# Slots for expert weights given back in pieces before the first expert product, the residual products all behind it, one router product split around a transpose

## The reference

```python
h = h + mixer_block(rmsnorm(h, norm1_g[l]), ...)      # ends with: return merged @ w_o
h = h + hier_moe(rmsnorm(h, norm2_g[l]), w_group[l], w_router[l], w1[l], w3[l], w2[l])

# hier_moe: logits of 8 groups and 64 experts, the best group, its two best experts, then for each
return (jax.nn.silu(xb @ w1[e]) * (xb @ w3[e])) @ w2[e]
```

## Time and profile before

| | us |
|---|---|
| median of 3 runs | 1562.71 (1562.51 to 1564.31) |
| profiled execution, its own time | 1561.92 |
| its span | 1560.1 |
| PE busy in the span | 1263.3 (81%) |
| DMA share and rate, mean from 700 to 1500 us | 1.01, 428 GB/s |
| last landing of expert weights | 1551.5 |

### The profile page before, as it was taken

One profiled execution on the slowest core, in us unless ns is written; L12 is line 12 of the kernel. 1 busy time (PEld: TensorE's weight loads), 2 busy tenths in 40 slices (PEclk: granted clock), 3 DMA queues, 4 the chain that ended last, 5 costly groups with the idle time before them and its releaser, 6 DMA issues.

```text
span 1560.1 us, 16698 instructions
## 1 busy us (share of the span) xinstructions
PE 1263.3 (81%) x6953; PEld 642.1 (41%) x6953; DVE 516.9 (33%) x1096; ACT 228.8 (15%) x649; POOL 17.8 (1%) x30
## 2 busy tenths in 40 slices
PE   9999999999999999997676576577576576476577
PEld 4665644444588544543232232223233223223223
DVE  6554577785453674311011111111111111111101
ACT  2435213111122101211001001001001001001001
POOL 2000000000000000100000000000000000000000
PEclk9999999999999999999788888788888789788889
DMA  9531756405433449899999999999999999999997
GB/s 302 210 114 55 245 155 205 155 35 216 157 113 109 166 157 370 347 429 428 428 429 428 429 427 430 427 428 428 429 428 428 428 428 429 427 428 429 429 426 323
DMA packets 93419, 501.40 MB, mean 321 GB/s; under 512 B 6797, under 2 KB 34817, under 8 KB 68160
## 3 DMA queue, kind: packets, MB, share of 16 engines
q1 hardware_dynamic: 92608, 500.00, 78.9%
q0 software_dynamic: 768, 0.85, 0.3%
HBM read 499.78 MB, written 1.05 MB: 321 GB/s over the span
## 4 chain that ended last, share of the span: by engine, by line
PE 58%; DMA 39%; DVE 1%; issue 0%; SPq 0%; ACT 0%; DVEq 0%
DMA arena<-in_w 38%; PE ps L1630 17%; PE ps L1253 8%; PE ps L862 7%; PE ps L1505 6%; PE ps L1305 3%; PE ps L857 2%; PE ps L1067 2%; PE ps L1557 2%; PE ps L907 2%; PE ps L1437 2%; PE ps L1207 1%; DMA arena<-in_w_in 1%; PE ps L1375 1%; PE ps L1280 1%
## 5 line engine op out<-in xcount | busy, mean ns | idle before, releaser
L1630 PE MATMUL ps<-arena,hT 128*32 128x512 f32 x1984 | 276.9, 721 | 255.4 <-DMA arena<-in_w 255.4
L1630 PEld LDWEIGHTS ps<-arena,hT 128*32 128x32 f32 x1984 | 69.2, 130 | 462.6 <-issue 319.8
L2722 DVE TENSOR_TENSOR moe_hid<-moe_hid,ps 64x512 f32<-64x512 f32 x32 | 22.1, 690 | 482.8 <-ACT moe_hid L3090 482.8
L1652 PE MATMUL ps<-arena,moe_turned 128*32 128x512 f32 x1024 | 116.7, 595 | 28.0 <-DVE moe_turned L2724 27.8
L1610 PEld LDWEIGHTS ps<-sel,h 128*128 128x128 f32 x992 | 113.2, 192 | 24.1 <-issue 24.1
L1610 PE MATMUL ps<-sel,h 128*128 128x64 f32 x992 | 117.2, 276 | 0.0
L3090 ACT ACTIVATE moe_hid<-ps 64x512 f32<-64x512 f32 x32 | 18.8, 588 | 656.2 <-PE ps L1630 650.5
L862 PE MATMUL ps<-hT,arena 128*128 128x256 f32 x512 | 113.9, 380 | 0.1
L862 PEld LDWEIGHTS ps<-hT,arena 128*128 128x128 f32 x512 | 96.8, 190 | 15.0 <-issue 2.2
L3074 ACT ACTIVATE hT<-ps,gcol 128x64 f32<-128x64 f32 x252 | 55.0, 328 | 158.5 <-PE ps L1610 156.8
L1505 PE MATMUL ps<-arena 128*128 128x512 f32 x176 | 77.3, 593 | 0.0
(11 more groups left out here) (465 smaller groups left out, 1245.4 us busy)
## 6 DMA issues: line engine op xcount, KB each, us to landing
arena<-in_w SPq DMA_DIRECT2D x184, 2048.0 KB, 29.3
arena<-in_w_in SPq DMA_DIRECT2D x18, 2048.0 KB, 8.5
arena<-in_w_up SPq DMA_DIRECT2D x22, 1024.0 KB, 9.4
arena<-in_w SPq DMA_DIRECT2D x14, 1024.0 KB, 13.2
arena<-in_w_down SPq DMA_DIRECT2D x5, 2048.0 KB, 13.7
arena<-in_w_out SPq DMA_DIRECT2D x2, 2048.0 KB, 14.3
arena<-in_w_conv_out SPq DMA_DIRECT2D x2, 2048.0 KB, 7.8
arena<-in_w_attn_out SPq DMA_DIRECT2D x2, 2048.0 KB, 7.8
```

Of the source, the lines that this page charges most:

```text
L1630: last = mm(ps[k * CAP:(k + 1) * CAP, UP, :], x[:, c, (k % 2) * CAP:(k % 2 + 1) * CAP], w[:, at:at + DE], start=(c == 0), stop=(c == KC - 1))
L1652: last = mm(ps[k * CAP:(k + 1) * CAP, DN, :], a[:, m * 64 + (k % 2) * CAP:m * 64 + (k % 2 + 1) * CAP], w[:, at:at + 512], start=(m == 0), ...
```

## The change

It does five things.

1. The loads of slots 0, 1 and 2 are issued ahead of `wao0`, `wao1`, `wo0` and `wo1` and no longer behind them.
2. `mrg` is laid out by halves of the tokens, so that the part of half 0 is free after `wo(0, 1)`. A quarter of slot 9 is loaded from then on (behind a wait on `bank_filled`), and another quarter with the rest.
3. `wo(1, 1)` raises `dense_used` once more in its middle, so that the first half of `wo1`'s place (slot 8) can be loaded from then on; the counts that others wait for go up by one.
4. The residual of half 0 is no longer taken from `h_res` by two products between the router's, but from `h` by two more products behind `first_up` (`take_residual`). The rest of slot 10 waits for `h_turned` in place of `res_taken`.
5. Of the router product `logits(1, 0)` two chunks come ahead of `turn_h(1, 1)` and two behind it.

```diff
@@ SP queue
-            static_units(UNIT["downC"], len(UNITS))
+            static_units(UNIT["downC"], UNIT["wao0"])
...
                     sp.wait_ge(rms_ready, 8)
                     sp.wait_ge(h_moved, 4)
-                    sp.wait_ge(res_taken, 1)
+                    sp.wait_ge(h_turned, 4)
                 else:
-                    sp.wait_ge(dense_used, released(UNIT[{3: "wao0", 4: "wao1", 7: "wo0", 8: "wo1", 9: "wo1"}[at]]))
+                    sp.wait_ge(dense_used, released(UNIT[{3: "wao0", 4: "wao1", 7: "wo0", 8: "wo1", 9: "wo1"}[at]]) + (at >= 8))
...
+            for k in range(3):
+                moe_wait(0, k)
+                load_quarter(MOE_SLOTS[k], k)
+            static_units(UNIT["wao0"], len(UNITS))
             for pair in range(PAIRS):
-                for k in (0, 1, 2, 4, 5, 3) if pair in (1, 2) else range(UNITS_PAIR):
+                for k in (0, 1, 2, 4, 5, 3) if pair in (1, 2) else range(0 if pair else 3, UNITS_PAIR):
                     if (pair, k) == (1, 1):
-                        load_part(4, 1)
-                        load_part(5, 0)
+                        load_part(4, 2048, 4096)
+                        load_part(5, 0, 2048)
+                        sp.wait_ge(bank_filled, filled(PROD["wo_h0"], 1))
+                        load_part(4, 0, 1024)
                     if pair == 1 and k in (4, 5):
                         moe_wait(pair, k)
-                        load_part(k, k - 4)
+                        load_part(k, *((1024, 2048), (2048, 4096))[k - 4])
                         continue
...
+                    if (pair, k) == (1, 2):
+                        at = moe_slot(1, 2)
+                        sp.wait_ge(dense_used, released(UNIT["wo1"]))
+                        sp.dma_start(MOE_SLOTS[at][:, 0:2048], t["w3"][2, :, 0:2048]).then_inc(moe_loaded[at], 16)
+                        moe_wait(1, 2)
+                        sp.dma_start(MOE_SLOTS[at][:, 2048:4096], t["w3"][2, :, 2048:4096]).then_inc(moe_loaded[at], 16)
+                        continue
@@ PE: wo, logits, residual
-                    last = mm(ps[:, BANKS[step][n], :], mrg[:, c, half * P:(half + 1) * P], slot_view(u)[:, c, :],
+                    last = mm(ps[:, BANKS[step][n], :], mrg[:, half, c, :], slot_view(u)[:, c, :],
                               start=(c == 0), stop=(c == KC - 1))
+                    if half and n and c == 3:
+                        last.then_inc(dense_used, 1)
...
-            logits(1, 0)
+            logits(1, 0, (0, 1))
             turn_h(1, 1, (4, 3))
+            logits(1, 0, (2, 3))
             pe.wait_ge(assigned, 1)
...
+            def take_residual(half, n):
+
+                rows = h[:, half, :].rearrange("p (c n) -> p n c", c=KC)[:, n * 64:(n + 1) * 64, :]
+                mm(ps[:, 2 * half + n, :], ident, rows, start=True, stop=False, skip_group_check=True)
...
-            mm(ps[:, 0, :], ident, h_res[:, 0, 0:512], start=True, stop=False, skip_group_check=True)
...
-            mm(ps[:, 1, :], ident, h_res[:, 0, 512:1024], start=True, stop=False, skip_group_check=True).then_inc(res_taken, 1)
...
                 if p == 0:
-                    for n in range(2):
-                        rows = h[:, 1, :].rearrange("p (c n) -> p n c", c=KC)[:, n * 64:(n + 1) * 64, :]
-                        mm(ps[:, 2 + n, :], ident, rows, start=True, stop=False, skip_group_check=True)
+                    for half in range(2):
+                        for n in range(2):
+                            take_residual(half, n)
```

More of the change, by code:

```diff
@@ L391, in two_blocks @@
         w_sum_b = b1(4, 512)
-        mrg = xn2.rearrange("p a b -> p (a b)").rearrange("p (c s) -> p c s", c=KC)
+        mrg = xn2.rearrange("p h (c s) -> p h c s", c=KC)
         def down_at(i):
@@ L456, in moe_count @@
         def moe_count(slot, turn):
-            return 16 * turn + ((48 if turn == 1 else 64) if slot == 0 else 16 if slot in (1, 2, 3, 9, 10) else 0)
+            return 16 * turn + ((48 if turn == 1 else 64) if slot == 0 else 32 if slot == 9 else 16 if slot in (1, 2, 3, 8, 10) else 0)
         xg = hT[:, :, 0:2 * CAP]
@@ L562, in two_blocks @@
         piece_in = sem("piece_in")
-        quarter_used, res_taken = sem("quarter_used"), sem("res_taken")
+        quarter_used = sem("quarter_used")
         SEL_FIRST, SCATTERED_FIRST = PAIRS + 1, PAIRS + 1
@@ L706, in moe_wait, with load_part @@
                     sp.wait_ge(h_moved, 4)
-                    sp.wait_ge(res_taken, 1)
+                    sp.wait_ge(h_turned, 4)
                 else:
-                    sp.wait_ge(dense_used, released(UNIT[{3: "wao0", 4: "wao1", 7: "wo0", 8: "wo1", 9: "wo1"}[at]]))
-            def load_part(k, part):
+                    sp.wait_ge(dense_used, released(UNIT[{3: "wao0", 4: "wao1", 7: "wo0", 8: "wo1", 9: "wo1"}[at]]) + (at >= 8))
+            def load_part(k, lo, hi):
                 at = moe_slot(1, k)
-                sp.dma_start(MOE_SLOTS[at][:, part * 2048:(part + 1) * 2048], t["w2"][k - 2, :, part * 2048:(part + 1) * 2048]
-                             ).then_inc(moe_loaded[at], 16)
+                sp.dma_start(MOE_SLOTS[at][:, lo:hi], t["w2"][k - 2, :, lo:hi]).then_inc(moe_loaded[at], 16)
+            for k in range(3):
+                moe_wait(0, k)
+                load_quarter(MOE_SLOTS[k], k)
+            static_units(UNIT["wao0"], len(UNITS))
             for pair in range(PAIRS):
-                for k in (0, 1, 2, 4, 5, 3) if pair in (1, 2) else range(UNITS_PAIR):
+                for k in (0, 1, 2, 4, 5, 3) if pair in (1, 2) else range(0 if pair else 3, UNITS_PAIR):
                     if (pair, k) == (1, 1):
-                        load_part(4, 1)
-                        load_part(5, 0)
+                        load_part(4, 2048, 4096)
+                        load_part(5, 0, 2048)
+                        sp.wait_ge(bank_filled, filled(PROD["wo_h0"], 1))
+                        load_part(4, 0, 1024)
                     if pair == 1 and k in (4, 5):
                         moe_wait(pair, k)
-                        load_part(k, k - 4)
+                        load_part(k, *((1024, 2048), (2048, 4096))[k - 4])
                         continue
@@ L1566, in turn_h, with logits @@
                 last.then_inc(h_turned, 1)
-            def logits(half, n):
+            def logits(half, n, chunks=range(4)):
                 if n:
@@ L1575, in logits @@
                     pe.wait_ge(hT_act, 21 + half)
-                for c in range(4 * n, 4 * n + 4):
+                for c in (4 * n + k for k in chunks):
                     last = mm(ps[:, 6 - half, 0:NG + NE], hT[:, c, half * P:(half + 1) * P], router_w[:, c, :],
@@ L3043, in _ @@
                 act.wait_ge(m_turned, k + 1)
-                a_(mrg[:, 4 * n:4 * n + 4, half * P:(half + 1) * P], ps[:, bank, :].rearrange("p (c s) -> p c s", c=4),
+                a_(mrg[:, half, 4 * n:4 * n + 4, :], ps[:, bank, :].rearrange("p (c s) -> p c s", c=4),
                    ACT.Copy).then_inc(mrg_ready, 1)
```

## The result

| | before | changed |
|---|---|---|
| median of 10 runs each, us | 1563.03 (1562.22 to 1564.31) | 1567.95 (1566.1 to 1572.14) |
| profiled execution, its own time, us | 1561.92 | 1567.15 |
| its span, us | 1560.1 | 1565.4 |

The ratio is 1.0030, 95% interval 1.0022 to 1.0039. I had forecast 1562.2 (1560.8 to 1564.3), which is 0.5 us faster: wrong in sign, and the change is ten times that size. Timed again beside the experiments, the kernel before lay above 1565.5 in 20 of 96 runs, so the size of the loss is less sure than its sign.

The account below looks back on a forecast made before the run. Expert-weight reading was taken as the bound, with the 16th piece's landing deciding. Slot 4's later release (687.5 against 688.0) outweighed piece 12's 1.2 us, leaving -0.5 us: median 1562.2, range 1560.8 to 1564.3.

Parts of the forecast that it names:

- What bounds the kernel: Reading of expert weights from about 663 us: the end is the 16th piece's landing plus 863.5 plus 8.6 us.
- Slots 0 to 2 ahead of `wao0`: Early loads of 6.3 MB, moved from behind 592 to behind 544 us: gain 0, cost 0, 14.7 us become idle DMA.
- The cover: Second `wao` load, behind the early loads, would land at 576 to 577, 2.5 us ahead of DVE's need at 579.5.
- Pieces: Slots 8 to 10 in at about 657.6, not 662.2; gain given back before `first_up`, 0.8 us left at piece 12.
- The residual products: Two taken out of the router: 0.3 us gained ahead of `gather_first(1)`, 0 for L1679; both come back behind `first_up`.
- +3.63 us on PE ahead of slot 4: Four products behind `first_up` take 7.26 us, not 3.63; slot 4 issued at 679.7, piece 16 landing at 687.5, not 688.0.
- theory 2: Experiments' theory: the four products behind `first_up` delay slot 4's release by 3.5 us, more than its load's queue covers.
- The divided router product: In the router: `turn_h` 0.3 us earlier, but ACT's copy only ends at 650.8; gain 0.1 us (0 to 0.3).
- Slot 4 comes late: Rival at the 16th piece's issue: own load time above 8.3 us, up to 1.3 us slower, 1564.0; chance 0.13.
- front counts: Rival at 640 to 660 us: loads, not places, caused the gap; closing it gains 5.3 us, 1557.4; chance 0.07.
- cheap restart: Rival at slot 4: own load time below 7.1 us, the whole 1.2 us of piece 12 stay, 1561.5; chance 0.10.
- `wao` late: Rival at the second `wao` load: costs only from 2.5 us late, then hidden by 10; part of the remaining chance.

Follow-up runs that it names:

- e4: Kernel before with only the loads of slots 0 to 2 issued ahead of `wao0`; 1563.47 us, ratio 1.0000.
- e5: Changed kernel plus two filling products in PE's router waits, all four residual products moved behind `expert_down` of pair 0; 1563.51 us, ratio 0.9996.
- e8: Changed kernel plus one unneeded product of constants in PE's longer wait, for DVE's choice of experts; 1564.53 us, ratio 1.0006.
- e10: Changed kernel plus one filling product in PE's longer wait, all residual products behind `expert_down` of pair 0; 1563.53 us, ratio 0.9997.
- e9: Changed kernel plus one unneeded product only in the short wait ahead of the second `gather_first`, the longer wait left empty; 1570.4 us, ratio 1.0030.
- e1: Changed kernel plus two unneeded products of constants where the residual products of half 0 stood in the router; 1564.88 us, ratio 1.0006.
- e6: Kernel before with two more residual products behind `first_up` (those of half 1 done twice); 1564.21 us, ratio 1.0004.
- e3: Kernel before with only the residual of half 0 moved behind `first_up`, slot 10 waiting for `h_turned`; 1566.98 us, ratio 1.0031.
- e7: Kernel before with half 0's residual products moved from the router to behind `expert_down` of pair 0, slot 10 waiting for `h_turned`; 1567.27 us, ratio 1.0017.
- e2: Changed kernel with half 0's residual back between the router's products and slot 10's rest waiting for it; 1562.36 us, ratio 0.9993.
- e11: Kernel before with one filling product in PE's longer wait, all residual products late, slot 10 waiting for `h_turned`; 1564.12 us, ratio 1.0001.

## Why the prediction was wrong, point by point

- **What bounds the kernel.** Right. In all thirteen profiles the last landing follows the 16th by 862 to 865 us. The tail of 8.6 us is less fixed: 8.6 to 10.5.
- **Slots 0 to 2 ahead of `wao0`: gain 0, cost 0.** Right (e4: 1.0000). The idle DMA stands at 600 to 610 with 28 GB/s. The cover was thinner than I had it: the second `wao` load landed 10.3 us after its issue at 569.7, at 580.0, and DVE used it at 581.3, 1.3 us later and not 2.5.
- **Pieces: gain ahead given back, 0.8 us left at piece 12.** The first half is right, the gap is now behind 660. The slots were all in at 659.7 (after, less 1.83) and not at 657.6, without effect. The gain at piece 12 was 0.5 to 0.6 in e5 and e8; with PE cured it is lost at the 14th piece, and the 16th lands where it did before (e5, e10).
- **The residual products: the step that failed.** I wrote of the first of them "The other one (L1679) ran while PE waited for DVE: 0", and of the second "gain 0.3 us". The term that failed is the 0 for L1679. That instruction was free in time, but not in effect: it kept PE's clock up (e8 against e9). Without it the clock fell to 0.50 and took 1.95 us in `gather_first` and 1.23 us in `first_up`, 3.2 us in the profile of after; the ratios of the changed kernel and e1 give 3.7. The gain of the other product is confirmed: 0.45, where I had 0.3. I had costed a removal by its duration and by who waits for it, and had not asked what the engine does in the time left empty. The page "TensorE: Matmul & The Clock Gate" of the Trainium skill, section "Part 1: The HAM clock gate (the "warmup" mystery)", says that the throttled clock is the default and that activity releases it. The fall to 0.50 in after and the 1.00 in e1 agree with that.
- **+3.63 us on PE ahead of slot 4, hidden but for 0.5.** Right in size of the products (7.08 for four, forecast 7.26). The time from issue to landing, for which I took the 7.8 us of a lone load, was 8.6 in after, 8.3 in e6, 9.3 in e1, 9.5 in e3 and e7, 10.0 in e8. In these six the load was not alone: slot 3's second load, issued ahead of it, landed 2.2 to 4.6 us after slot 4's was issued. In e9, where it had just landed, it was 7.5. So the price of a lone load was right, and what I had wrong is that slot 4's would be one. By the ratios of e1 and e8 against e5 and e10 it cost 1.4 to 1.6 us, within intervals that overlap; by e6 0.6. So theory 2 is the smaller part, and its size is not clear of the noise.
- **The divided router product: 0.1 us.** PE now waits 0.17 us for ACT's copy and no longer 0.40 for DVE's, but it goes on at 652.77, less 1.83 at 650.94, where it was 650.95 before: gain 0.0.
- **The sum.** By the profile: +1.83 (early fall), -0.45 (product gone), +3.18 (clock), +3.45 (two more products), together 8.0 us later at slot 4's issue (684.5 - 676.5); less 2.9 of queue (11.5 - 8.6) gives the 5.1 of the landing. I had 3.2 of these 8.0. Without the early fall the landing is 3.3 us later, while the medians lie 4.9 apart; the falls of e7 and e9, which are longer than that of after, show that it has no fixed size, but which of them the other runs of after had is not known.
- **The rivals.** "Slot 4 comes late" had the sign and the place, with a price of 1.3; "front counts" is refuted by e5, and "cheap restart", which wanted less than 7.1 us, by the 7.5 of e9. No rival had the clock. And the chances of the four cases add up to 1.00, so that the fifth, "`wao` late", had none of its own.

Open: the 1.83 us at 95 us are in the profiled execution of after and not in that of before, and I can't say how often either kernel has them; the ratios take them as spread.

## What to carry to other kernels

Ask of every instruction that is taken out of an engine's wait what the engine does instead; on PE, work in a wait can be worth more than its own time. Ahead of a stage bound by transfers, earlier loads paid here only as far as the next places came free earlier too: find the piece whose place comes last, and follow its release, not the gap in the rates. Price a moved instruction at both ends. Before a load is priced as a lone one, look when the load ahead of it lands.

## What the runs showed of the hardware

- In every profile in which PE's wait of 1.2 us for the choice of experts was left empty (after, e3, e7, e9) the granted clock fell from 1.00 to 0.50: at about 657.7 in after and 655.6 in e7, between 0.2 us ahead of that wait's end and 0.7 us behind it, and ahead of the second wait where there was one. With one product of 1.0 to 1.1 us in the first wait it stayed at 1.00 there in all nine others (before, e1, e2, e4, e5, e6, e8, e10, e11).
- PE was busy nearly all the time after the fall, and still the clock stayed down until 664.5 in after, 664.3 in e3, 665.8 in e7 and 667.6 in e9. At the lower clock the second `gather_first` took 3.68 in place of 1.73 us.
- By the times of e9 the fall comes in most runs, not in all. In e7 and e9 a second one came at `expert_down` (5.34 in place of 3.64 us), behind a wait of 0.8 us that the kernel before has without a fall. So the length of a wait alone does not settle it.
- A 2 MB load took 7.5 us from issue to landing at slot 4 when nothing was ahead of it (e9), and 8.3 to 10.0 when the load before it had still 2.2 to 4.6 us to its own landing (after, e1, e3, e6, e7, e8).
